# A 31-tap causal convolution as products of even and odd tokens with stored four-tap matrices, in place of diagonal products and vector taps

## What is computed

```python
def conformer_conv(u, conv_dw, conv_b, ln_g, ln_b, conv_pw):
    a, g = jnp.split(u, 2, axis=-1)
    y = a * jax.nn.sigmoid(g)
    y = lax.conv_general_dilated(
        y, conv_dw[:, None, :], window_strides=(1,), padding=[(CONV_KERNEL - 1, 0)],
        dimension_numbers=('NWC', 'WIO', 'NWC'), feature_group_count=CONV_WIDTH)
    y = y + conv_b
    y = jax.nn.silu(layernorm(y, ln_g, ln_b))
    return jnp.einsum('bsc,cd->bsd', y, conv_pw)
...
def first_block(...):
    for i in range(DEPTH):
        a = rmsnorm(h, norm_mix_pre[i])
        u = jnp.einsum('bsd,de->bse', a, w_in[i])
        q, k, v, qi, ki, wi, u_conv, u_pool = jnp.split(u, IN_SPLITS, axis=-1)
        ...
        y_attn = dsa_sparse_attention(q, k, v, qi, ki, wi)
        y_conv = conformer_conv(u_conv, ...)
        y_pool = multiscale_pool(u_pool, pool_w[i], pool_scale[i])
        mix = jnp.concatenate([y_attn, y_conv, y_pool], axis=-1)
        mix = jnp.einsum('bse,ed->bsd', mix, w_out[i])
        ...
```

## Time and profile before

| | us |
|---|---|
| median of 3 runs | 2365.07 (2364.63 to 2365.8) |
| the profiled execution's own time | 2364.69 |
| span of the profiled execution | 2362.9 |
| PE busy | 2336.6 (99%) |
| DVE busy | 1550.3 (66%) |
| ACT busy | 1194.3 (51%) |
| POOL busy | 118.8 (5%) |

### The profile page before, as it was taken

How to read it: one execution, slowest core, us unless ns; L and a number is a source line. 1 busy time by engine, 2 the same in 40 slices (tenths; PEclk the granted TensorE clock), 3 DMA queues, 4 the chain that set the end, 5 groups by cost and what they waited for, 6 DMA issues and landing times.

```text
span 2362.9 us, 30405 instructions
## 1 busy us (share of the span) xinstructions
PE 2336.6 (99%) x12096; PEld 1981.5 (84%) x12096; DVE 1550.3 (66%) x2041; ACT 1194.3 (51%) x1734; POOL 118.8 (5%) x223
## 2 busy tenths in 40 slices
PE   7999999999999999999999999999999999999998
PEld 6888888888888888988888888888889888888887
DVE  6866567866656656776485666665567765856664
ACT  6445446445445546545344455554565454444553
POOL 0500000500000000000000000000000000000000
PEclk9999999999999999999999999999999999999999
DMA  7236656236556665554656465565565445564563
GB/s 273 81 104 205 208 187 213 73 108 214 185 175 227 198 196 179 195 167 159 199 178 202 160 213 180 179 229 195 182 196 193 160 165 191 182 207 162 190 194 126
DMA packets 117501, 427.11 MB, mean 181 GB/s; under 512 B 13296, under 2 KB 13552, under 8 KB 117104
## 3 DMA queue, kind: packets, MB, share of 16 engines
q1 hardware_dynamic: 117360, 425.16, 54.7%
HBM read 424.05 MB, written 1.05 MB: 180 GB/s over the span
## 4 chain that ended last, share of the span: by engine, by line
PE 88%; DVE 6%; POOL 2%; DMA 1%; ACT 1%; issue 1%; SPq 0%; DVEq 0%; POOLq 0%; ACTq 0%
PE ub L1632 21%; PE ub L1636 11%; PE ub L1610 8%; PE ub L1612 8%; PE ub L1611 8%; PE acc L1610 8%; PE acc L1612 8%; PE acc L1611 8%; DVE wlo L946 2%; DMA raw<-in_w 1%; PE acc L1929 1%; POOL tapd L415 1%; DVE XN L987 1%; PE acc L2042 1%; ACT junk L512 1%
## 5 line engine op out<-in xcount | busy, mean ns | idle before, releaser
L946 DVE TENSOR_TENSOR wlo<-raw,whi 128x1024 fp32r<-128x1024 f32 x776 | 916.7, 1222 | 246.1 <-ACT whi L490 244.2
L490 ACT ACTIVATE whi<-raw 128x1024 fp32r<-128x1024 f32 x776 | 782.8, 1053 | 259.4 <-PE ub L1612 148.5
L1632 PE MATMUL ub<-xhl,whi 128*128 128x512 f32 x2176 | 595.2, 395 | 0.0
L1632 PEld LDWEIGHTS ub<-xhl,whi 128*128 128x128 f32 x2176 | 375.5, 189 | 53.5 <-issue 1.0
L1636 PEld LDWEIGHTS ub<-xhl,wlo 128*128 128x128 f32 x2176 | 333.5, 189 | 46.2
L1636 PE MATMUL ub<-xhl,wlo 128*128 128x256 f32 x2176 | 345.8, 281 | 0.0
L1610 PE MATMUL acc<-whi,bhl 128*128 128x512 f32 x736 | 288.6, 392 | 0.0
L1612 PE MATMUL acc<-whi,bhl 128*128 128x512 f32 x736 | 287.5, 391 | 0.0
L1611 PE MATMUL acc<-wlo,bhl 128*128 128x512 f32 x736 | 287.2, 390 | 0.0
L1610 PE MATMUL ub<-whi,xhl 128*128 128x512 f32 (+1 forms) x704 | 275.6, 391 | 7.8 <-DVE wlo L946 4.3
L1611 PE MATMUL ub<-wlo,xhl 128*128 128x512 f32 (+1 forms) x704 | 272.8, 387 | 0.0
(11 more groups left out here) (311 smaller groups left out, 2578.5 us busy)
## 6 DMA issues: line engine op xcount, KB each, us to landing
raw<-in_w SPq DMA_DIRECT2D x776, 512.0 KB, 4.9
gain<-in_gains SPq DMA_DIRECT2D x20, 512.0 KB, 8.2
par<-in_par SPq DMA_DIRECT2D x2, 1068.0 KB, 9.4
DEC<-in_decay SPq DMA_DIRECT2D x2, 768.0 KB, 7.3
H<-in_x SPq DMA_DIRECT2D x2, 512.0 KB, 6.1
out_h<-H SPq DMA_DIRECT2D x4, 256.0 KB, 2.3
par<-in_par SPq DMA_DIRECT2D x2, 419.0 KB, 8.2
PT<-in_p SPq DMA_DIRECT2D x2, 256.0 KB, 8.4
```

The source lines that it names most:

```text
L490: do(act.activation(whi[:, s % RING, c], raw[:, s % RAW, c], ACT.Copy), counts["w_hi"])
L946: do(dve.tensor_tensor(wlo[:, s % RING, c], raw[:, s % RAW, c], whi[:, s % RING, c].bitcast(f32), ALU.subtract), counts["w_lo"])
L1632: pe.matmul(bank, whi[:, s % RING, n:n + P], xhl[:, kt, :, :].rearrange("p a n -> p (a n)"), start=kt == 0, stop=False, skip_group_check=True)
```

## The change

The tokens are taken in pairs. `YC` now has one row for each parity of the token (rows 0 to 63 even, 64 to 127 odd) and each of 64 channels, for 4 groups of channels, and 15 + 128 columns. One 128x128 matrix holds, for a group and a shift of whole pairs, the weights that lead from the even and odd input to the even and odd output, four at most for a channel. There are 16 such shifts for each of 4 groups: 64 products of 128 columns instead of 46 of 256 columns, one with the unit matrix, and 16 multiply-adds on DVE.

- The matrices are laid out on the host (`shifts`) and loaded by SP in 8 pieces of 512 KB a layer into a ring of four places, `tapw`, that lie in four different stretches of memory used by other tiles before. POOL writes no diagonals.
- The convolution's input is projected with tokens in the rows (`conv_in`: two chunks for each half of the tokens, 12 products of 512 columns for each chunk and half). DVE gates a half of the tokens at a time and writes it twice (`YT`, 512 columns), PE transposes it (`turn_conv`, 8 transposes, between the two halves of the pool's product), and ACT takes the even and the odd tokens out of it (`even_and_odd`, 4 copies of 64 rows by 256).
- 24 taps stand ahead of the heads (14 before), and 8 in each of the first five heads (7, 7, 6, 6, 6 before).
- Mean, variance and scale are made in the new layout; the variance comes as one number a token, without a diagonal. `conv_out` is 16 products of 64 rows by 128 columns instead of 4 of 128 rows by 256. `par1`, loaded once a layer, grows from 838 to 1294 columns.

```diff
-TAPS_BEFORE, TAPS_AFTER = 14, (7, 7, 6, 6, 6)
+TAPS_BEFORE, TAPS_AFTER = 24, (8, 8, 8, 8, 8)
...
+        tapw = [sb(f"tapw{n}", 0, at=unit(u), shape=[P, PIECE, P]) for n, u in enumerate((32, 4, 12, 16))]
...
+                def load_taps(L, first, end):
+
+                    for n in range(first, end):
+                        k = PIECES * L + n
+                        if n >= TAP_RING:
+                            sp.wait_ge(sem["tap_used"], k - TAP_RING + 1)
+                        sp.dma_start(tapw[n % TAP_RING][:, :, :].rearrange("p a n -> p (a n)"),
+                                     a["taps"][k * P:(k + 1) * P, :]).then_inc(sem[f"tap_in{n % TAP_RING}"], 16)
...
+                        if s == s1(L, "inp", 10):
+                            if L:
+                                sp.wait_ge(sem["split_free"], s1(L - 1, "ple") + 1)
+                            load_taps(L, 0, 1)
+                        if s == s1(L, "out", 2):
+                            sp.wait_ge(sem["ze"], 7 * L + 5)
+                            load_taps(L, 1, 2)
+                            sp.wait_ge(sem["dots_done"], IDX_HEADS * (L + 1))
+                            load_taps(L, 2, 5)
+                        if s == s1(L, "out", 3):
+                            load_taps(L, 5, 6)
+                        if s == s1(L, "ffn"):
+                            load_taps(L, 6, PIECES)
...
-                    def sigmoid(f):
-                        used(s0 + 8 + f)
-                        do(act.activation(tS[:, f, 0:S], acc[:, f, S:2 * S], ACT.Sigmoid), counts["act_out"])
+                    def sigmoid(t):
+                        if t:
+                            used(s0 + 9)
+                        else:
+                            nxt("cz")
+                        do(act.activation(tS[:, t, 0:S], acc[:, 3 * t, S:2 * S], ACT.Sigmoid), counts["act_out"])
...
-                    def gated(f):
+                    def gated(t):
+
                         nxt("act_out")
                         settle()
-                        do(dve.tensor_tensor(YC[:, f, TAPS - 1:], acc[:, f, 0:S], tS[:, f, 0:S], ALU.mult),
-                           counts["in_free"])
+                        x, y = (z.rearrange("p (g d) -> p g d", d=64).unsqueeze(2).broadcast_to([P, GROUPS, 2, 64])
+                                for z in (acc[:, 3 * t, 0:S], tS[:, t, 0:S]))
+                        do(dve.tensor_tensor(YT[:, t, :, :, :], x, y, ALU.mult), counts["in_free"])
...
-                            own_taps(k0, k0 + 4)
...
+                    def conv_in(part, t):
+
+                        s = s0 + 8 + part
+                        if part == 0:
+                            fill(A_[3 * t], "in_free")
+                        last = wide_block(s, 4 * part, t, acc[:, 3 * t, :], part == 0, part == 1, xhi, xlo)
+                        if t:
+                            give(last)
+                        elif part:
+                            give(last, "cz")
...
+                    def turn_conv():
+
+                        pe.wait_ge(sem["in_free"], 3 * L + 2)
...
                     dots(7, 10)
-                    pair_in(s0 + 8, 0, 0)
+                    conv_in(0, 0)
                     dots(10, 13)
-                    pair_in(s0 + 8, 0, 1)
+                    conv_in(0, 1)
                     dots(13, 16)
-                    for f in range(2):
-                        pair_in(s0 + 9, 1, f)
+                    conv_in(1, 0)
+                    conv_in(1, 1)
                     turn_in(3)
-                    for f in range(2):
-                        pair_in(s0 + 10, 2, f)
+                    pool_in(0)
+                    turn_conv()
+                    pool_in(1)
...
+                            if k == 0:
+                                pe.wait_ge(sem[f"tap_in{piece % TAP_RING}"], 16 * (2 * L + piece // TAP_RING + 1))
+                            last = pe.matmul(acc[:, 3, cols(g)], tapw[piece % TAP_RING][:, k, :], YC[:, g, q:q + PAIRS],
+                                             start=q == 0, stop=q == SHIFTS - 1)
```

More of the change, by code:

```diff
@@ L397, in _ @@
                 do(pool.memset(half[:, :], -0.5))
-                do(pool.memset(means[:, :], 1.0 / 256))
+                do(pool.memset(means[:, :], 0.0))
+                settle()
+                do(pool.memset(means[0:64, 0:64], 1.0 / 256))
+                do(pool.memset(means[64:P, 64:P], 1.0 / 256))
                 settle()
@@ L1951, in _ @@
                             fill(A_[3], "ha_ready")
-                            for k in range(2):
-                                last = pe.matmul(acc[:, 3, 0:S], means[:, :], cacc[:, k, :], start=k == 0, stop=k == 1)
+                            for g in range(GROUPS):
+                                last = pe.matmul(acc[:, 3, 0:PAIRS], means[:, :], cacc[:, g, :],
+                                                 start=g == 0, stop=g == GROUPS - 1)
                             give(last, "mean_done")
@@ L1966, in _ @@
                             fill(A_[3], "var_ready")
-                            for k in range(2):
-                                last = pe.matmul(acc[:, 3, 0:S], means[:, :], tS[:, 0, k * S:(k + 1) * S], start=k == 0, stop=k == 1)
+                            for g in range(GROUPS):
+                                last = pe.matmul(acc[:, 3, 0:2], tS[:, 0, cols(g)], means[:, 0:P:64],
+                                                 start=g == 0, stop=g == GROUPS - 1)
                             give(last, "stat_done")
@@ L1982, in conv_out @@
                         nxt("sig_ready")
-                        U_[1].take(pe, sem["prod_ready"], 4 * L + 4)
+                        for place_ in U_[0:2]:
+                            place_.take(pe, sem["prod_ready"], 4 * L + 4)
                         for f in range(2):
-                            for k in range(2):
-                                c = P1["conv_pw"] + (k * 2 + f) * P
-                                last = pe.matmul(ub[:, 1, f * S:(f + 1) * S], par1[:, c:c + P], cact[:, k, :],
-                                                 start=k == 0, stop=k == 1)
+                            for g in range(GROUPS):
+                                for j in range(2):
+                                    r = slice(64 * j, 64 * j + 64)
+                                    c = P1["conv_pw"] + (g * 2 + f) * P
+                                    last = pe.matmul(ub[:, j, f * PAIRS:(f + 1) * PAIRS], par1[r, c:c + P],
+                                                     cact[r, g, :], start=g == 0, stop=g == GROUPS - 1)
                         give(last, "aux_ready")
@@ L2232, in block_chunks, with twice, shifts @@
     return m.reshape(k // 512, 4, P, n // 512, 512).transpose(3, 0, 2, 1, 4).reshape(-1, P, CHUNK)
+def twice(v):
+    v = v.reshape(GROUPS, 64, -1).transpose(1, 0, 2).reshape(64, -1)
+    return np.concatenate([v, v], axis=0)
+def shifts(dw):
+    out = np.zeros((GROUPS, SHIFTS, 2, 64, 2, 64), np.float32)
+    c = np.arange(64)
+    for q in range(SHIFTS):
+        for i in range(2):
+            for j in range(2):
+                k = 2 * q + i - j
+                if 0 <= k < TAPS:
+                    out[:, q, i, c, j, c] = dw[k].reshape(GROUPS, 64)
+    out = out.reshape(PIECES, PIECE, P, P).transpose(0, 2, 1, 3)
+    return np.ascontiguousarray(out).reshape(PIECES * P, PIECE * P)
 def in_order(parts, order):
@@ L2239, in lay_out @@
 def lay_out(v):
-    w, par1, par2, ps, gains = [], [], [], [], []
+    w, par1, par2, ps, gains, taps = [], [], [], [], [], []
     heads = [half * 4 + f for f in range(4) for half in range(2)]
@@ L2250, in lay_out @@
         w_out = w_out.reshape(KT, P, D)[list(OUT_ORDER)].reshape(D, D)
-        w += [block_chunks(m) for m in (first, qi[:, 0:512], qi[:, 512:], q)]
-        w += [chunks(tiles(np.concatenate(last, axis=1))), column_chunks(w_out)]
+        w += [block_chunks(m) for m in (first, qi[:, 0:512], qi[:, 512:], q, conv)]
+        w += [chunks(tiles(pool)), column_chunks(w_out)]
         w += in_order({"first": block_chunks(v["w_up"][l][:, 0:1024]), "up": chunks(tiles(v["w_up"][l])),
```

159 lines of the change are left out of this document (73 added, 86 removed).

## The result

| | before | after |
|---|---|---|
| median (us) | 2364.86, 6 runs (2364.17 to 2365.8) | 2372.97, 6 runs (2369.01 to 2374.57) |
| profiled execution's own time | 2364.69 | 2371.62 |
| its span | 2362.9 | 2369.8 |
| mean granted clock | 1.0 | 0.996 |

The change made the kernel slower: ratio 1.0032, 95% interval 1.0021 to 1.0042, or about 8 us. The forecast was 2359.9 in a range of 2357.5 to 2365.5, so the result lies outside it. The spread of the runs grew too, from 1.6 to 5.6 us.

What follows compares the result with a forecast made beforehand. PE, busy 99% of the span, was taken as the bound. Per layer 3.4 - 7.0 + 0.7 + 0.3 = -2.6 us, -5.2 in all, giving a median of 2359.9 us, range 2357.5 to 2365.5.

Steps and rivals of the forecast that it cites:

- the clock behind the wait for the gating: Rival: PE's clock falls in its wait for the second gating, costing 2.5 us a layer; chance 0.18.
- the wait for piece 6: PE's wait in the heads for tap piece 6, wanted at 112.1, landed at 112.8: +0.7 us a layer, between 0 and 2.
- Up to the second gating: Layer 0 from chunk s0+8: first gating starts at 82.3, second runs from 88.85 to 89.55.
- PE's wait: PE idles 4.4 us, from 85.2 to 89.6, for the second gating, after half of the pool's chunk.
- To the first head: Transposes, pool's second half, two heads' scores and 24 taps put the first head's transposes at 99.6 against 96.19: +3.4 us.
- The heads: Old taps, unit matrix and a diagonal wait leave PE (-15.9), 40 new taps at 0.22 add 8.9: -7.0 us a layer.
- Landing takes 3.8 alone and 512 KB / 404 GB/s = 1.3 more behind the chunk's half: Step timing piece 6's DMA: asked for at 108.1, it lands at 112.8.
- conv_out: conv_out's 16 smaller products, taken with the layer norm: +0.3 us a layer.
- par1: The larger par1 load at the start was taken as 0, at most +0.6 us, once.
- Weight loads that don't overlap the products: Rival: weight loads set the taps' pace, 0.38 or more a tap, 10 us more a layer, 2380; chance 0.05.

Runs made afterwards that it cites:

- e1: Changed kernel plus 18 needless products of 128 columns on PE just ahead of its wait for the second gating: 2373.24 us, ratio 1.0040.
- e2: Changed kernel with the first sigmoid moved behind the rectified scores of heads 13 to 15 in ACT's list: 2365.53 us, ratio 1.0007.
- e9: e3 with the needless products of e1 in PE's wait for the second gating: 2365.11 us, ratio 0.9999.
- e3: Changed kernel with tap pieces 6 and 7 asked for ahead of chunk s0+15 instead of behind it: 2365.54 us, ratio 1.0001.
- e4: Changed kernel with the first load of par1 asked for behind chunk 6 instead of ahead of chunk 2: 2372.66 us, ratio 1.0032.
- e12: Changed kernel with 32 taps ahead of the heads, 8 in each of four, pieces 4 to 7 asked for ahead of chunk s0+14: 2365.91 us.
- e13: e12 plus the needless products of e1 in PE's wait for the second gating: 2361.45 us, ratio 0.9985.
- e14: e11 without its conv_out edit, so conv_out waits for all four silus again: 2352.63 us, ratio 0.9950.
- e6: Changed kernel with the edits of e2 and e3, pieces 4 to 7 not loaded and 0 to 3 reused (wrong output): 2354.99 us.
- e11: e12 plus e2's edit, gated-input transposes behind the whole pool product, and conv_out's first half waiting silu by silu: 2350.03 us, ratio 0.9941.

## Why the prediction was wrong, step by step

Forecast was a gain of 5.2 us in the profiled execution; it lost 6.9. Two terms failed most: the clock behind the wait for the gating, which the sum had at nothing, and the wait for piece 6 with the clock behind it, which it had at 0.7 a layer.

- **Up to the second gating: right.** First gating forecast at 82.3, measured 83.04; the second forecast to end by 89.55, and PE took it at 90.33. Of both differences 0.7 is the later start. Its 512 columns took 0.69, for the 0.70 taken.
- **PE's wait: right.** 4.4 forecast; 4.23 and 4.24.
- **To the first head: the mechanism right, the sum wrong.** From the transposes to the first head 10.0 were forecast (89.6 to 99.6; the terms named add up to 9.9); it took 10.50 at full clock (e1, e2, e9), 12.87 and 11.76 in the changed kernel. The failed step is "Whether a wait of 4.4 us is enough to lose the clock no row shows. I keep it as a rival at 2.5 a layer", with a chance of 0.18. The clock fell in all eight waits of this length (two each of the changed kernel, e3, e4 and e12). Its price was sized well: 2.4 and 1.3 in the changed kernel, 2.2 a layer from e12 and e13, against 2.5. (The slow start from which the 2.5 was read is a reading of the spacing alone: the clock column of the earlier trace rows shows 1.00 from 10 to 15.) The argument against it, a full list of PE work on both sides, bore no weight.
- **The heads: nearly right.** 24 taps took 5.46 to 5.75 where 5.3 were forecast, 8 in a head 1.85 to 1.9 instead of 1.76 (40 of these are 8.8, where the sum has 8.9). Over 64 taps that is some 0.4 to 0.9 a layer.
- **Piece 6: the place right, the size wrong.** +0.7 forecast, 2.10 and 2.66 measured, and 1.55 more for the clock behind the second. The failed step is "Landing takes 3.8 alone and 512 KB / 404 GB/s = 1.3 more behind the chunk's half". SP asked for it at 111.61, 3.5 later than forecast because all was later by then; it was there 6.7 us after that instead of 5.1, with two halves of a chunk ahead of it and piece 7 behind it. The DMA moved 309 to 350 GB/s there (last column), not 404:

```profile
114.00:116.00 2.00, 2.00 (x15) 1.50 (x14) 0.56 (x1) 0.49 (x1) 0.00 (x0) 1.00 0.97 309
116.00:118.00 2.00, 0.19 (x2) 0.05 (x1) 2.00 (x4) 0.99 (x4) 0.00 (x0) 1.00 0.87 350
```

- **conv_out: too small.** From the first product of the output projection to the end of `conv_out` it took 8.45 before (128.97 to 137.42) and 9.37 after (131.68 to 141.05): 0.9 a layer against 0.3. The products of `conv_out` are 0.4 of it. The wait for the silus is 0.98 instead of 0.21 (four of them take 1.65 where two took 1.09); I hadn't costed it. It adds 0.8, of which 0.2 comes back from the product that spreads the scale, which has half the columns (0.39 for 0.60). Before:

```profile
135.80 1.96 PE L1987 MATMUL ub<-cact,par 128*128 128x256 f32 x8 [0.21 <-issue]
137.42 0.58 PE L1610 MATMUL acc<-whi,bhl 128*128 128x512 f32 x1
```

- **par1: nothing,** as forecast (e4).
- **Weight loads that don't overlap the products: not so, as forecast.** A tap took 0.23, not 0.38.

In the profile after, layer 0 adds up. The first product of the output projection was forecast 2.9 earlier (126.1 for 128.97). To that come the later start 0.7, the clock 2.4, slower transposes and taps 0.5, the piece and the heads' taps 2.0, 5.6 in all: 2.7 later, as measured (131.68). `conv_out` brings 0.9 more, 3.6 in all. Layer 1 adds 3.95 (351.45 - 347.50), 6.5 above its forecast: there the clock is 1.3, the piece 2.0 and the clock behind it 1.55, slower transposes and taps in all 1.0, `conv_out` 0.6. The two layers are 7.6, and some 0.7 of it is regained behind the stage: 6.9, the difference of the spans. The sum had no row in which a wait costs more than its own length, and here both did, in the clock behind them. The first wait didn't make piece 6 late: PE wanted the piece 4.1 later than forecast (116.2 for 112.1), and SP asked for it only 3.5 later. With the first wait shorter (e2) or filled (e1), the piece's grew to 3.1 and 3.3.

## What to carry to other kernels

A new wait on a busy TensorE is to be costed with the clock behind it when the chain of work has nothing to put there; ask first what real work can stand in it (here the pool's second half and eight taps), since needless products keep the clock but not the time of the wait itself (e13 against e14). When a stage has two losses in a row, the second can take back what mending the first wins: the same products in the wait were worth nothing with late pieces (e1) and 4.5 us without them (e13 against e12). So judge an edit only where nothing behind it is late. When loads of two kinds share a queue in order, the place of each request among the others, and which engine waits for it with what behind it, can decide more than the bytes: the same pieces asked for elsewhere were worth 7.4 us here (e3).

## What the runs showed of the hardware

- **Waits and the clock.** Behind waits of PE of 4.2 us the granted clock fell every time (8 of 8); behind waits for pieces of 2.2 to 3.6 us in 7 of 7; behind 2.10 it stayed; behind 1.0 to 1.7 us it fell in 3 of 18 (1.03, 1.39 and 1.64), and behind the silus' 0.95 to 0.98 in none of 22. What sets the lower cases apart these runs don't tell. The runs of e6, e11, e13 and e14, whose profiles have neither a wait for a transfer nor one of 4 us in this stage, lie within 1.4 to 2.2 us of each other; those of the other changed kernels within 3.9 to 11.1. The Trainium skill (TensorE: Matmul & The Clock Gate, The HAM clock gate) says that the clock falls after an idle stretch; the traces agree, and show that one wait in a full list of work is enough.
- **A small exact product has a floor.** 128 columns took 0.114 a record in the taps, and products of 2 columns hardly less: eight records in 0.87 after (0.109 each), where four records of 256 columns take 0.92 (L1968 before). Each record has a weight load of its own; whether the load or the product sets the 0.11, no run here tells. The row after:

```profile
130.14 1.00 PE L2004 MATMUL acc<-means,tS 128*128 128x2 f32 x8
131.01 0.41 PE L1937 MATMUL acc<-V,work 128*128 128x64 f32 x2
```

- **Weight loads of 0.19 overlap products 0.11 apart.** Rows of the tap products after, in nanoseconds min/median/max, both over the same rows of the array. The rule that the prediction weighed, by which the Trainium skill (TensorE: Matmul & The Clock Gate, What overlaps and what doesn't) lets loads overlap running products only where the row groups differ, doesn't agree with that:

```profile
L1966 PEld LDWEIGHTS acc<-YC,tapw x128: 186/192/192, 97.7 to 123.8; 128*128 128x128 f32 x128
L1966 PE MATMUL acc<-YC,tapw x128: 273/275/377, 97.7 to 123.9; 128*128 128x128 f32 x128
```
